# Norm sums and norm spread placed between the last row blocks of a stage's head; decay series moved into the first MLP; VectorE's first rotation product placed ahead of its wait

## The reference, cut to what matters

```
for layer in (0, 1):
    h = rmsnorm(x, g)                    # mean of squares over the 1024 features, per token
    x = x + mixer(h)                     # layer 0 "even": windowed attention with rotations, and pooling
                                         # layer 1 "odd": latent attention with rotations, and a gated recurrence
    x = x + relu(rmsnorm(x, g2) @ W1)**2 @ W2       # 1024 -> 4096 -> 1024
x = rmsnorm(x, g_final)
...                                      # second model: norm, wide projection, attention, output
```

## Time and profile before

| | us |
|---|---|
| median of 3 runs | 1485.85 (1485.76 to 1486.09) |
| time of the profiled execution | 1486.7 |
| its span | 1484.9 |
| PE busy in it | 1441.6 (97%) |
| DVE busy | 779.6 (53%) |
| ACT busy | 604.2 (41%) |
| POOL busy | 597.5 (40%) |

### The profile page before, as it was taken

The page is one execution under the profiler, slowest core; times in us unless marked ns, Lnnn a source line. Parts: engine busy times, 40 slices in busy tenths (PEclk is TensorE's granted clock), DMA queues, the critical chain, the costliest instruction groups (busy, mean ns, idle before and its releaser), DMA issues.

```text
span 1484.9 us, 20275 instructions
## 1 busy us (share of the span) xinstructions
PE 1441.6 (97%) x7064; PEld 1137.9 (77%) x7064; DVE 779.6 (53%) x1389; ACT 604.2 (41%) x1092; POOL 597.5 (40%) x332
## 2 busy tenths in 40 slices
PE   6989999999999999999999999999999999999996
PEld 5667878888888888556878888888877877776885
DVE  6874552223444577896542223444477547676434
ACT  5444432232222345965422223222263435654432
POOL 3433254444444445511544444444424642222440
PEclk9999999999999999999999999999999999999998
DMA  5212232222222222210222222222213321121221
GB/s 219 71 58 76 81 113 99 91 93 100 99 99 99 93 78 86 71 44 15 86 99 90 94 99 99 99 99 93 90 59 128 137 104 58 57 72 44 72 71 57
DMA packets 36625, 129.56 MB, mean 87 GB/s; under 512 B 4048, under 2 KB 4176, under 8 KB 36560
## 3 DMA queue, kind: packets, MB, share of 16 engines
q1 hardware_dynamic: 35136, 124.80, 24.2%
q10 hardware_dynamic: 1424, 3.90, 0.7%
HBM read 126.58 MB, written 2.10 MB: 87 GB/s over the span
## 4 chain that ended last, share of the span: by engine, by line
PE 57%; issue 25%; POOL 12%; DVE 4%; ACT 2%; DMA 0%; POOLq 0%; ACTq 0%; DVEq 0%; SPq 0%
PE bank L668 16%; PE bank L670 15%; PE bank L669 15%; POOL w L650 12%; PE bank L777 3%; PE bank L802 2%; PE bank L821 2%; PE bank L1124 1%; PE bank L737 0%; DVE rms L1687 0%; DVE tmp L1767 0%; PE bank L726 0%; DVE opC L1655 0%; DVE arena L2234 0%; DMA raw<-stream_dram 0%
## 5 line engine op out<-in xcount | busy, mean ns | idle before, releaser
L650 POOL TENSOR_TENSOR w<-raw,w 128x1024 fp32r<-128x1024 f32 (+1 forms) x328 | 597.3, 1836 | 854.3 <-ACT w L1233 472.5
L668 PE MATMUL bank<-opC,w 128*128 128x512 f32 x624 | 253.3, 406 | 13.8 <-DVE opC L1655 10.4
L670 PE MATMUL bank<-opC,w 128*128 128x512 f32 x624 | 245.3, 393 | 0.0
L669 PE MATMUL bank<-opC,w 128*128 128x512 f32 x624 | 244.6, 392 | 0.0
L1819 DVE TENSOR_TENSOR mlp_op<-arena,mlp_op 128x512 fp32r<-128x512 f32 x64 | 144.4, 2259 | 188.7 <-ACT mlp_op L1353 188.7
L1325 ACT ACTIVATE w<-raw 128x1024 fp32r<-128x1024 f32 x126 | 133.2, 1057 | 239.5 <-PE bank L670 239.5
L668 PE MATMUL bank<-mlp_op,w 128*128 128x512 f32 x544 | 211.9, 389 | 1.5 <-ACT arena L1446 1.5
L669 PE MATMUL bank<-mlp_op,w 128*128 128x512 f32 x544 | 211.7, 389 | 0.0
L670 PE MATMUL bank<-mlp_op,w 128*128 128x512 f32 x544 | 211.6, 389 | 0.0
L668 PE MATMUL bank<-opA,w 128*128 128x512 f32 x416 | 162.8, 391 | 2.2 <-DVE arena L1814 1.4
L1812 DVE TENSOR_TENSOR tmp<-tmp,rms 128x512 f32<-128x512 f32 x64 | 51.5, 804 | 211.0 <-ACT tmp L1333 210.6
(11 more groups left out here) (231 smaller groups left out, 1897.6 us busy)
## 6 DMA issues: line engine op xcount, KB each, us to landing
raw<-stream_dram SPq DMA_DIRECT2D x232, 512.0 KB, 3.4
out_t_dram<-arena SPq DMA_DIRECT2D x8, 256.0 KB, 2.2
x<-x_t_dram SPq DMA_DIRECT2D x4, 256.0 KB, 5.6
x<-x_t_dram ACTq DMA_DIRECT2D x4, 256.0 KB, 6.9
rope<-ropes_dram ACTq DMA_DIRECT2D x2, 512.0 KB, 6.7
con<-consts_dram ACTq DMA_DIRECT2D x1, 993.5 KB, 8.0
arena<-p_t_dram ACTq DMA_DIRECT2D x1, 512.0 KB, 3.7
par<-params_dram ACTq DMA_DIRECT2D x1, 253.5 KB, 3.8
```

The costliest lines, as they stand in the source:

```text
L650: low = pool.tensor_tensor(w_lo[:, j, part], raw[:, j, part], w_hi[:, j, part].bitcast(F32), ALU.subtract)
L668: pe.matmul(out, wh, hi, start=first, stop=False)
L669: pe.matmul(out, wh, lo, start=False, stop=False)
L670: return pe.matmul(out, wl, hi, start=False, stop=last)
```

## The change

`head` takes `norm_sums` behind row block 5 (`HEAD_SUMS`) and `norm_spread` behind row block 6 (`HEAD_SPREAD`) of its eight; for norm "final" the sums stay behind row block 7 and the spread where it was. The calls of `norm_spread` behind the heads go. The two early rotations of PE stand before row blocks 1 and 3 of the fourth tile. `rotate` on DVE waits for its tile (`z_ready`) ahead of the first product, and for PE's matmul (`rot_full`) only ahead of the second. `log_decay` is cut into two parts, of 15 and 13 instructions, which follow the low parts of the third and the fourth hidden tile of `down0`. The arithmetic is the same.

```diff
+HEAD_SUMS, HEAD_SPREAD = 5, 6
...
                         if k == KT - 1:
                             mm.then_inc(acc_full, 1)
-                if after_down:
-                    pe.wait_ge(z_ready, t0)
-                if stage == "ein":
-                    pe.wait_ge(con_in, 16)
-                norm_sums(norm)
+                    if k == (KT - 1 if norm == "final" else HEAD_SUMS):
+                        if after_down:
+                            pe.wait_ge(z_ready, t0)
+                        if stage == "ein":
+                            pe.wait_ge(con_in, 16)
+                        norm_sums(norm)
+                    if k == HEAD_SPREAD and norm != "final":
+                        norm_spread(norm)
...
                 head(f"up{layer}", op, op, after_down=True)
-                norm_spread(op)
...
             head("ein", "even", "even")
-            norm_spread("even")
...
             for k in range(E_AHEAD):
-                if k in (2, 5):
+                if k in (1, 3):
                     rotate_even(k // 3)
                 e_product("ein", HEAD, k)
...
             head("oin", "odd", "odd", after_down=True)
-            norm_spread("odd")
...
-                if before_spread:
-                    before_spread()
                 if name != "final":
                     spread(name)
...
-            def rotate(n, tile, m, b, scratch):
-
-                dve.wait_ge(rot_full, n + 1)
+            def rotate(n, tile, ready, m, b, scratch):
+
+                dve.wait_ge(z_ready, ready)
                 if n:
                     dve.wait_ge(roped, n)
                 one, two = (t[0:m, :] for t in scratch)
                 mark(TTn(one, tile[0:m, :], rope[0:m, 0, :], ALU.mult))
+                dve.wait_ge(rot_full, n + 1)
                 step(TTn(two, bank[b][0:m, :], rope[0:m, 1, :], ALU.mult))
...
                 for j in range(2, RING):
                     low_part(0, j)
+                    if layer == 0:
+                        log_decay(j - 2)
```

More of the change, by code:

```diff
@@ L1687, in add_square, with norm @@
                     TTn(total, total, new, ALU.add).then_inc(sq_used, 1)
-            def norm(name, gain, ready=None, taken_from=None, before_spread=None):
+            def norm(name, gain, ready=None, taken_from=None):
                 ahead = {"down0": 2, "down1": 2, "eout": 1, "oout_b": 1}.get(taken_from, 0)
@@ L1800, in group_bank, with log_decay, horner @@
                 return bank[out_bank(family, k)]
+            def log_decay(part):
+                terms = 10
+                def horner(first, last):
+                    for k in range(first, last - 1, -1):
+                        step(TTn(small[:, 6, :], small[:, 6, :], small[:, 5, :], ALU.mult))
+                        step(TS(small[:, 6, :], small[:, 6, :], 1.0 / (2 * k + 1), None, ALU.add))
+                if part == 0:
+                    dve.wait_ge(lam_act, 2)
+                    step(TS(small[:, 2, :], small[:, 1, :], 2.0, None, ALU.add))
+                    step(nc.vector.reciprocal(small[:, 3, :], small[:, 2, :]))
+                    step(TTn(small[:, 4, :], small[:, 3, :], small[:, 1, :], ALU.mult))
+                    step(TTn(small[:, 5, :], small[:, 4, :], small[:, 4, :], ALU.mult))
+                    step(TS(small[:, 6, :], small[:, 5, :], 1.0 / (2 * terms + 1), 1.0 / (2 * terms - 1), ALU.mult, ALU.add))
+                    horner(terms - 2, 4)
+                else:
+                    horner(3, 0)
+                    step(TTn(small[:, 7, :], small[:, 6, :], small[:, 4, :], ALU.mult))
+                    step(TS(small[:, 8, :], g("lam", 0, 8), -1.0, 0.0, ALU.mult, ALU.max))
+                    step(STT(small[:, 9, :], small[:, 7, :], 2.0, small[:, 8, :], ALU.mult, ALU.add))
+                    TS(small[:, 14, :], small[:, 9, :], -LRU_C, None, ALU.mult).then_inc(sp_made, 1)
+                    TS(small[:, 15, :], small[:, 9, :], -LRU_C / 2, None, ALU.mult).then_inc(sp_made, 1)
             def mlp(layer):
@@ L1847, in cut_conv @@
                         step(ins)
[L1849 to L1866, removed]
             dve.wait_ge(par_in, 16)
@@ L1874, in _ @@
                 nc.vector.memset(pool_in[i][:, SEQ + 8:], 0.0)
-            norm("even", "g_even", lambda m: dve.wait_ge(x_in[m], 16), before_spread=log_decay)
+            norm("even", "g_even", lambda m: dve.wait_ge(x_in[m], 16))
             def rotate_even(n):
-                rotate(n, z0(EVEN_ROTATED[n]), P, (2, 3, 1, 0, 1)[n], (more[:, 2, :], more[:, 3, :]))
+                i = EVEN_ROTATED[n]
+                rotate(n, z0(i), TILE0["ein"] + EIN.index(i) + 1, P, (2, 3, 1, 0, 1)[n], (more[:, 2, :], more[:, 3, :]))
             dve.wait_ge(rope_in, 16)
@@ L2003, in _ @@
             dve.wait_ge(rope_in, 32)
-            rotate(5, key_rope, P, 2, (tmp[:, 2, :], tmp[:, 3, :]))
+            rotate(5, key_rope, TILE0["oin"] + 4, P, 2, (tmp[:, 2, :], tmp[:, 3, :]))
             scaled("oin", 7, z1(OIN[7]))
@@ L2025, in _ @@
             lru_scan(2, part_scanned)
-            rotate(6, mla["qr"][0], P, 3, (tmp[:, 2, :], tmp[:, 3, :]))
+            rotate(6, mla["qr"][0], TILE0["mq"] + 1, P, 3, (tmp[:, 2, :], tmp[:, 3, :]))
             def behind_mla(step):
@@ L2040, in behind_mla @@
                 if step == 5:
-                    rotate(7, mla["qr"][1], P, 1, (more[:, 2, :], more[:, 3, :]))
+                    rotate(7, mla["qr"][1], TILE0["mv"] + 7, P, 1, (more[:, 2, :], more[:, 3, :]))
                 if step in (4, 7, 8, 10, 11):
```

## The result

| | before | changed |
|---|---|---|
| median of 4 runs, us | 1485.91 | 1477.18 |
| lowest to highest | 1485.76 to 1486.09 | 1476.82 to 1480.55 |
| ratio, 95% interval | | 0.9945 [0.9933, 0.9956] |
| profiled execution, us | 1486.7 | 1480.55 |
| its span, us | 1484.9 | 1478.7 |

The change makes the kernel 8.7 us faster by the medians. The forecast was 1477.7. The profiled execution is the slowest of the four, 3.4 us above the median, so the sum has to be read stage by stage.

What follows compares the result with a forecast made beforehand. PE, busy 97% of the span, was taken to bound the kernel, so only its waits could go: 2.6 + 1.3 + 3.2 + 1.1 = 8.2 us off the 1485.85 median gives 1477.7 us, own range 1476.7 to 1479.0.

Steps and rivals of the forecast that it cites:

- Sums and spread, 0.64 us per head: In four heads, placing both between products avoids PE's wait on the reciprocal: 0.64 us each, 2.6 us in all.
- The margin of 1.4 us: In a head, the reciprocal would be ready 1.4 us before PE finishes row block 6 and takes the spread.
- the reciprocal would be wanted at about 30: In ein, the unmoved decay series would end at about 30.9 us, the reciprocal behind it wanted at about 30.
- ein, 0.64 + 1.3 = 1.9: In ein, 0.64 us from sums and spread, 1.3 us from the waits at the two early rotations.
- to cost the later rotations at nothing: In ein, later rotations find PE's matmul already there or follow DVE's work without idling: no cost.
- nothing would be given back: Behind each place of gain, what follows waits on PE's own output, so none of the 8.2 us returns.
- up0 and up1, 3.8 with their heads: In both MLPs, earlier eviction ends the fifth tile's wait and slow restart: 3.2 us, besides 0.64 us per head.
- The first rival for this place: In the MLPs, POOL still holds DVE's square, the fifth tile waits: 3.2 us not gained, 1480.9 us; chance 0.16.
- oin, 0.64 + 1.1 = 1.7: In oin, 0.64 us from sums and spread, 1.1 us from the fifth tile's wait for weights and its restart.
- Decay series in down0 at nothing: In down0, POOL holds one small instruction per part, yet low parts come in time, 0.9 us to spare: no cost.
- The squares' cover, 1.4 and 1.15 us: Squares are ready before PE's earlier sums, by 1.4 us in up0 and 1.15 us in oin: no cost.
- Rival three: At PE's sums behind row block 5, a late eighth square costs 2.1 us per head, 1490.3 us; chance 0.05.

Runs made afterwards that it cites:

- (3, 6): The changed kernel with sums behind row block 3 instead of 5, spread still behind row block 6: 1488.58 us, ratio 1.0018 against the kernel before.

## Why the prediction was right

The mechanism held: the waits went where they were forecast to go. The forecast of 8.2 us is met nearly stage by stage. That the median of the first four times, 1477.18, lies so near 1477.7 is in part luck: three of the four are in the lower of two groups. The median of all 14 times of this kernel is 1479.2, just above the forecast's own range of 1476.7 to 1479.0, by a scatter that the sum does not have.

- **Sums and spread, 0.64 us per head: right.** 0.81 and 0.81 us measured against 0.85 and 0.81, and all four waits for the reciprocal gone. The margin of 1.4 us was enough; with the series ahead of it, it would still have been (0.3 us). My sentence that the reciprocal would be wanted at about 30 missed that PE takes the spread only behind row block 6, nearly 3 us after the sums begin. It cost the forecast nothing.
- **ein, 0.64 + 1.3 = 1.9: measured 2.01.** The size is right, the split was not told: PE's places 0.69, DVE's order 0.26, and both need the earlier spread, without which they give 0.27 together. Wrong was to cost the later rotations at nothing: the third one takes 0.3 back, so the two stages together gain 1.7, and the sentence that nothing would be given back fails by that much.
- **up0 and up1, 3.8 with their heads: up0 2.18**, against 0.64 + 1.64 = 2.3 forecast, and 23.64 us against 23.5. The path was the forecast one: the square at 184.16 ahead of POOL's first low part at 185.75, the eviction through at 186.6, the early end of "186 to 189". The first rival for this place, that POOL outruns the spread, missed by the 0.9 us between the square's end and POOL's start. The restart is slow only before, behind the fifth tile's first matmul, and so outside these marks; up to the head of oin the gain is 2.33. For up1 the marks read 25.80 and 23.65, a gain of 2.15, and 0.15 more behind them for the restart.
- **oin, 0.64 + 1.1 = 1.7: measured 1.69.** ACT makes the fifth tile's weights at 536.17, 4.6 us before PE's fifth tile.
- **Decay series in down0 at nothing: right, to the instruction.** One small instruction of each part is held, and the steps stay 5.44 us apart (ACT's step ends, rows at 354.22 and 359.66):

```profile
354.22 1.06 ACT L1326 ACTIVATE w<-raw 128x1024 fp32r<-128x1024 f32 x1 [3.86 <-PE bank L671]
...
359.66 1.06 ACT L1326 ACTIVATE w<-raw 128x1024 fp32r<-128x1024 f32 x1 [3.86 <-PE bank L671]
```

```profile
355.45 2.34 DVE L1808 TENSOR_TENSOR small<-small 128x8 f32<-128x8 f32 x1
...
358.03 0.69 DVE L1844 TENSOR_TENSOR mlp_op<-arena,mlp_op 128x512 fp32r<-128x512 f32 x1
...
360.87 2.37 DVE L1824 TENSOR_SCALAR small<-small 128x8 f32<-128x8 f32 x1
```

  The fourth low part ends at 358.72, which is 360.8 on the clock of before (2.04 us later there): the forecast's number. A tensor_tensor and a tensor_scalar are held alike, 2.34 and 2.37 us. By the Trainium skill (GPSIMD Engine Reference, section 1, Specifications) the second, with one SBUF tile as input, would be so only in a two-port mode; these rows do not tell modes apart, and the sum does not depend on it.
- **The squares' cover, 1.4 and 1.15 us: right.** No wait with sums at 5; with 4, one row block of 2.04 us earlier, the waits are 0.62 and 0.88, which puts the margins at 1.42 and 1.16 us.
- **The price of a late square was too low.** Rival three reckoned waits alone, 2.1 us per head, and three heads; up1 had none even with the sums at 3. Where the waits were made that long, 2.7 and 2.9 us, the clock fell behind them and cost nearly as much again. My sum of 1482.8 for (3, 6) failed by this term; above 1483 stood there for a lower clock.

What I had not in the sum at all is the scatter. All 14 times of the changed kernel lie in two groups, five at 1476.8 to 1477.4 and nine at 1479.0 to 1480.6; the forecast of 1477.7 happens to stand between them. Profiles differ in four places: the start, by up to 1.5 us; the half-clock stretch in the attention, 1.5; the one near 1352, 1.6; and the end, from the last norm's sums on, 11.6 to 12.6 us. All three profiles of the changed kernel are of the upper group, so which of the four parts the groups is not shown. Whether the change makes that stretch more frequent stays open: the profile of before lacks it, but the version with sums and spread behind the head again, which has before's heads and time, has it too.

## What to carry to other kernels

A small reduction that another engine must finish goes between the products, early enough to cover the round trip and late enough for its inputs; the window between the two was two row blocks wide here, and each side was tried. The larger part of such a gain may lie not at the wait itself but in what is released earlier: of the 8.2 us forecast only 2.6 were sums and spread, the rest were rotations, evictions and weights that were ready before PE asked for them. A reordering that helps at one place is to be followed to the next wait: DVE's new order gained 0.26 us at the first scores and lost 0.3 at the third rotation. When medians scatter by more than the effect, measure stages between fixed marks of the trace.

## What the hardware showed unexpectedly

- A wait of PE of 2.07 us inside a stretch that is otherwise full is followed by 3.4 us at half the granted clock in some profiles and not in others. Twelve profiles have this wait at that place: behind it the clock fell in eight and stayed up in four, before among these. The stretch costs 1.5 us. Behind a wait of 1.92 us it fell too, behind 2.66 us for 6.8 us, behind 2.92 us for 3.4; behind 0.62, 0.88 and 0.94 us in the places tried here it did not. Near 1352 us, where waits of 0.88 and 0.66 us follow each other, it fell in two of the three profiles of one and the same program, the changed kernel.
- With the 2.07-us wait cut to 0.94 the median is 1475.4 us, against 1479.3 for the changed kernel in another batch. The shorter wait explains 0.8 of the 3.9, the missing stretch in the attention 1.5. The rest is not shown to come from the edit: the stretch near 1352 is missing in profiles of other versions too. That the fall stays away in all five executions is argued from one profile and the narrow times.
- DVE's held instructions are as long for 128x8 (2.34 to 2.38 us) as for 128x512 (2.17 to 2.48): beside a 128x1024 instruction of POOL (2.40 us) what is held lasts about until that one ends, not as long as its own work would. In down0 POOL's instruction ends at 357.76 and the held one at 357.79.
